# The first norm of the last layer in two halves of 128 columns, and the mean of every norm squared by ScalarE

## The reference, cut to what matters

```python
for i in range(DEPTH):                      # DEPTH = 4, D_MODEL = 1024
    last = i == DEPTH - 1
    h_lat = x_lat * (1.0 + m_lat[:, 1]) + m_lat[:, 0]
    h_ctx = x_ctx * (1.0 + m_ctx[1]) + m_ctx[0]
    y_lat, y_ctx = mixer(i, h_lat, h_ctx)   # attention or gated linear attention, then @ w_o
    x_lat = layer_norm(alpha * x_lat + m_lat[:, 2] * y_lat, ln1_g[i], ln1_b[i])
    h_lat = x_lat * (1.0 + m_lat[:, 4]) + m_lat[:, 3]
    f_lat = conv_ffn(h_lat, ffn_w_up[i], ffn_conv_w[i], ffn_conv_b[i], ffn_w_down[i])
    x_lat = layer_norm(alpha * x_lat + m_lat[:, 5] * f_lat, ln2_g[i], ln2_b[i])
    if not last:
        ...                                 # the same for the context

def layer_norm(x, g, b):                    # over the 1024 features of a token
    mu = mean(x); var = mean((x - mu) ** 2)
    return (x - mu) * rsqrt(var + LN_EPS) * g + b
```

## Time and profile before

| | us |
|---|---|
| median of three runs | 2580.01 |
| lowest and highest of them | 2573.11, 2580.82 |
| the profiled execution, its own time | 2578.89 |
| its span in the trace | 2577.1 |
| TensorE busy in it | 2438.4 (95 %) |
| VectorE busy | 1392.1 (54 %) |
| ScalarE busy | 1134.2 (44 %) |
| GpSimd busy | 334.9 (13 %) |

### The profile page before, as it was taken

One profiled execution on the slowest core, in us unless ns is written; L12 is line 12 of the kernel. 1 busy time (PEld: TensorE's weight loads), 2 busy tenths in 40 slices (PEclk: granted clock), 3 DMA queues, 4 the chain that ended last, 5 costly groups with the idle time before them and its releaser, 6 DMA issues.

```text
span 2577.1 us, 37987 instructions
## 1 busy us (share of the span) xinstructions
PE 2438.4 (95%) x15310; PEld 1960.5 (76%) x15310; DVE 1392.1 (54%) x2099; ACT 1134.2 (44%) x1936; POOL 334.9 (13%) x270
## 2 busy tenths in 40 slices
PE   6999899999999898999999999899999999978997
PEld 3655877778789558777788878787777888947997
DVE  2375665453444776555534336766555435477874
ACT  3375543333342565333323444454333325276663
POOL 0000311110100003111101003331111111002111
PEclk8999899999999999999999999999999999999998
DMA  7712366663232002665632421025666335603663
GB/s 246 213 42 81 92 182 186 180 178 105 78 99 88 28 25 66 187 181 180 176 104 80 112 69 43 2 67 150 186 185 181 113 92 105 149 17 101 186 180 99
DMA packets 500995, 311.39 MB, mean 121 GB/s; under 512 B 24194, under 2 KB 499762, under 8 KB 500692
## 3 DMA queue, kind: packets, MB, share of 16 engines
q1 hardware_dynamic: 498048, 307.39, 41.0%
q10 hardware_dynamic: 2772, 1.56, 0.2%
HBM read 307.87 MB, written 1.05 MB: 120 GB/s over the span
## 4 chain that ended last, share of the span: by engine, by line
PE 82%; DVE 7%; ACT 5%; DMA 3%; issue 2%; SPq 1%; ACTq 0%; DVEq 0%
PE bank L1543 69%; PE bank L1595 4%; PE bank L1722 2%; PE bank L1770 1%; DMA slab_raw<-in_d_w_qkv 1%; PE bank L1742 1%; DMA slab_raw<-in_a_w_o 1%; ACT slab_hi L526 1%; DVE stat L1184 1%; DVE slab_lo L960 1%; ACT p L707 1%; ACT hb L541 1%; DVE q_part L1243 1%; DMA slab_raw<-in_mod_w 1%; ACT pt L719 1%
## 5 line engine op out<-in xcount | busy, mean ns | idle before, releaser
L1543 PE MATMUL bank<-h_hi,slab_hi 128*128 128x512 f32 (+1 forms) x2416 | 859.6, 356 | 38.7 <-DVE slab_lo L960 26.5
L1543 PE MATMUL bank<-h_lo,slab_hi 128*128 128x512 f32 (+1 forms) x2416 | 836.9, 346 | 0.0
L960 DVE TENSOR_TENSOR slab_lo<-slab_raw,slab_hi 128x1024 fp32r<-128x1024 f32 (+1 forms) x388 | 538.6, 1390 | 552.1 <-ACT slab_hi L526 550.7
L1543 PE MATMUL bank<-h_hi,slab_lo 128*128 128x512 f32 (+1 forms) x2416 | 836.6, 346 | 0.0
L526 ACT ACTIVATE slab_hi<-slab_raw 128x1024 fp32r<-128x1024 f32 (+1 forms) x388 | 401.5, 1036 | 529.1 <-PE bank L1543 264.1
L1543 PEld LDWEIGHTS bank<-h_hi,slab_hi 128*128 128x128 f32 x2416 | 465.1, 193 | 150.0 <-issue 90.2
L1543 PEld LDWEIGHTS bank<-h_hi,slab_lo 128*128 128x128 f32 x2416 | 465.3, 193 | 55.9
L1543 PEld LDWEIGHTS bank<-h_lo,slab_hi 128*128 128x128 f32 x2416 | 465.9, 193 | 50.0 <-issue 0.5
L929 ACT ACTIVATE conv<-bank,prm 128x512 f32<-128x512 f32 (+1 forms) x176 | 127.3, 723 | 355.1 <-PE bank L1543 354.8
L1543 PE MATMUL bank<-g_hi,slab_hi 128*128 128x512 f32 (+1 forms) x770 | 269.3, 350 | 2.1 <-ACT res_t L577 2.1
L1543 PE MATMUL bank<-g_hi,slab_lo 128*128 128x512 f32 (+1 forms) x770 | 267.2, 347 | 0.0
(11 more groups left out here) (218 smaller groups left out, 2744.0 us busy)
## 6 DMA issues: line engine op xcount, KB each, us to landing
slab_raw<-in_mod_w SPq DMA_DIRECT2D x192, 512.0 KB, 4.5
slab_raw<-in_ffn_w_up SPq DMA_DIRECT2D x176, 512.0 KB, 4.6
slab_raw<-in_ffn_w_down SPq DMA_DIRECT2D x64, 512.0 KB, 4.1
slab_raw<-in_ffn_w_down SPq DMA_DIRECT2D x32, 384.0 KB, 3.5
slab_raw<-in_b_w_qkv SPq DMA_DIRECT2D x24, 512.0 KB, 3.8
slab_raw<-in_c_w_in SPq DMA_DIRECT2D x24, 512.0 KB, 3.8
slab_raw<-in_d_w_qkv SPq DMA_DIRECT2D x24, 512.0 KB, 7.0
slab_raw<-in_a_w_qkv SPq DMA_DIRECT2D x12, 512.0 KB, 5.4
```

Source lines behind the costliest of these rows:

```text
L960: nc.vector.tensor_tensor(wlo[slot][:, 0:w], raw[of][:, 0:w], whi[slot][:, 0:w].bitcast(f32), ALU.subtract).then_inc(s_lo, 1)
L1543: ins = mm(out, l, r, start=first and n == 0, stop=last and n == 2)
```

## The change

Three things are edited.

1. `halves(6)` becomes two parts, columns 256 to 383 and 384 to 511: the latents in two halves of 128. Stage 6 so takes the path with two parts: 4 tiles of the mixer's output projection for 256 columns, 4 tiles for the first 128, the same 4 for the other 128; `stats` twice, on 128 columns each; then `four_ahead` over the first four slabs of the MLP's up projection, for the first half of the columns and again for the second. `hb`, which holds 256 columns, is used as far as a part is wide. `segs` gives the columns of a part cut at 256, and its first number (which of the two modulation vectors) stays 1 for both halves. The code that took the single part of stage 6 through `modulate` and `last_part` goes.
2. In the block of TensorE, `whole` is counted anew for the stage behind the MLP, since stages 6 and 7 now differ.
3. In every norm ScalarE squares the mean straight from PSUM (`acc_s`), behind the copy of the mean, with a semaphore of its own; VectorE waits for it and subtracts `acc_s` from the mean square in PSUM. The instruction of L1015 is gone from VectorE. There are 15 norms of a part now, where there were 14.

```diff
 def halves(st):
-    return [slice(CTX, T)] if st // 2 == DEPTH - 1 else [slice(0, CTX), slice(CTX, T)]
+    if st == 2 * DEPTH - 2:
+        return [slice(CTX, CTX + P), slice(CTX + P, T)]
+    return [slice(CTX, T)] if st == 2 * DEPTH - 1 else [slice(0, CTX), slice(CTX, T)]
 def make_events(st):
     ...
-    return [Event(dt, slice(0, T), None, False) for dt in range(whole)] + [
+    return [Event(dt, slice(halves(st)[0].start, T), None, False) for dt in range(whole)] + [
...
         def segs(c):
-            return [s for s in ((0, slice(0, CTX)), (1, slice(CTX, T))) if s[1].start < c.stop and c.start < s[1].stop]
+            both = ((0, slice(0, CTX)), (1, slice(CTX, T)))
+            return [(s, slice(max(x.start, c.start), min(x.stop, c.stop))) for s, x in both if x.start < c.stop and c.start < x.stop]
...
             def normaliser(st, p):
                 c, n = halves(st)[p], parts_before(st, p) + 1
                 act.wait_ge(s_stats, n)
                 nc.scalar.activation(mean[:, c], LN_SUM[:, c], ACT.Copy).then_inc(s_mean, 1)
+                nc.scalar.activation(acc_s[:, c], LN_SUM[:, c], ACT.Square).then_inc(s_msq, 1)
                 act.wait_ge(s_var, n)
...
                 residual(st, fg)
-                if i + 1 == layers:
-                    for pr in range(PAIRS):
-                        modulate(st + 1, 0, pr)
...
             def variance(st, p):
                 c = halves(st)[p]
                 dve.wait_ge(s_stats, parts_before(st, p) + 1)
-                dve.wait_ge(s_mean, parts_before(st, p) + 1)
-                link(nc.vector.scalar_tensor_tensor(acc_s[:, c], mean[:, c], -1.0, mean[:, c], ALU.mult, ALU.mult))
-                link(nc.vector.tensor_tensor(acc_q[:, c], LN_SQ[:, c], acc_s[:, c], ALU.add))
+                dve.wait_ge(s_msq, parts_before(st, p) + 1)
+                link(nc.vector.tensor_tensor(acc_q[:, c], LN_SQ[:, c], acc_s[:, c], ALU.subtract))
                 nc.vector.tensor_scalar(acc_q[:, c], acc_q[:, c], 0.0, LN_EPS, ALU.max, ALU.add).then_inc(s_var, 1)
...
                 residual(st, start["wo", i][1])
-                if i + 1 == layers:
-                    last_part(st + 1, 0)
...
                 fg = start["down", i][1]
+                whole = sum(ev.part is None for ev in events[st + 1])
```

More of the change, by code:

```diff
@@ L310, in build_program @@
             "mean_ready", "var_ready", "rstd_ready", "centred", "xn_ready"))
+        s_msq = sem("mean_squared")
         s_cond_z, s_x1 = sem("cond_cleared"), sem("latents_modulated")
@@ L540, in modulate @@
                     for k in range(2):
-                        ins = nc.scalar.activation(hb[b][:, k, :], xn[:, 2 * pr + k, c], ACT.Identity,
+                        ins = nc.scalar.activation(hb[b][:, k, 0:c.stop - c.start], xn[:, 2 * pr + k, c], ACT.Identity,
                                                    bias=cf[:, 2 + s, 2 * pr + k:2 * pr + k + 1],
@@ L547, in modulate @@
                     act.wait_ge(s_x1, pr + 1)
-                nc.scalar.activation(h_hi[:, 2 * pr:2 * pr + 2, c], hb[b][:], ACT.Copy).then_inc(s_hhi, 1)
+                nc.scalar.activation(h_hi[:, 2 * pr:2 * pr + 2, c], hb[b][:, :, 0:c.stop - c.start], ACT.Copy).then_inc(s_hhi, 1)
             def normaliser(st, p):
@@ L1002, in rest @@
                 dve.wait_ge(s_hhi, n + 1)
-                nc.vector.tensor_tensor(h_lo[:, 2 * pr:2 * pr + 2, c], hb[n % 2][:],
+                nc.vector.tensor_tensor(h_lo[:, 2 * pr:2 * pr + 2, c], hb[n % 2][:, :, 0:c.stop - c.start],
                                         h_hi[:, 2 * pr:2 * pr + 2, c].bitcast(f32), ALU.subtract).then_inc(s_hlo, 1)
```

## The result

Slower, by more than forecast. The changed kernel takes **2599.66 us** (median of 7 runs, 2593.41 to 2602.76), beside 2580.82 us for the kernel before in as many (2573.11 to 2585.31): ratio **1.0071**, 95 % interval 1.0057 to 1.0086. Forecast were 2586.0 us and a range that ended at 2597; slower by over 0.3 % had a chance of 0.45, and no change 0.50. The profiled execution took 2600.32 us, 21.4 more than the 2578.89 of before; its span is 2598.5 us.

What follows compares the result with a forecast made beforehand. TensorE was taken as the bound, busy 95 % of the span. The halves' +13.9 us and the square's -6.9 us made +7.0 us on 2578.9, given as 2586 us, range 2572 to 2597.

Steps and rivals of the forecast that it cites:

- Part 1, the pace: Stage 6 and first four up slabs: 384 float32r matmuls of 128 columns, bounded by weight loads, 0.112 us each, 43.0 us.
- Rival A: Same stretch: a narrow float32r matmul is cheaper than a load alone, 0.06 to 0.09 us; kernel 2573 to 2579; chance 0.13.
- Rival B: Same stretch: narrow float32r matmuls fall to plain float32's 0.22 us each, needing a second pass; kernel about 2623; chance 0.16.
- Part 2, the waits: Stage 6 in halves: TensorE still waits 3.5 us (bounds 1 and 7.2); the second half's norm lies under matmuls.
- Part 2, the clock: Stage 6 in halves: a lower granted clock costs 1.0 us (0 to 2.5), sized by stage 2's stretch.
- Parts 1 and 2: Stretch from stage 6's output projection through the first four up slabs: 60.9 us against 47.0, +13.9 us.
- the two terms for a low clock: Stage 6's stretch: 1.0 us lost to a low clock after the change, 1.4 us lost before it.
- Part 3, the square: All norms: squaring the mean on ScalarE lets VectorE go on earlier; -6.9 us (-2 to -11).
- Rival C: All norms: the square gives nothing, as VectorE meets the next centring each time; kernel 2592; chance counted within the forecast's 0.68.
- The sum: Whole kernel: +13.9 us for the halves and -6.9 us for the square make +7.0 us, forecast 2586 us.

Runs made afterwards that it cites:

- e4: Kernel before, with layer 3's first four up slabs projected in halves of 128 columns (192 narrow matmuls for 96 wide ones): 2608.13 us, ratio 1.0118.
- e10: e4 with 17 idle matmuls ahead of the narrow ones and one ahead of each of the next two `h_lo` waits: 2586.47 us, ratio 1.0032.
- e11: Kernel before, with layer 3's first two up slabs left wide and the next four projected in halves of 128 columns: 2588.44 us, ratio 1.0039.
- e5: Changed kernel with one, two and two idle matmuls meant for the three waits inside stage 6's norm: 2578.95 us, ratio 1.0001.
- e6: e1 with 14 idle matmuls ahead of layer 3's first up pair, for stage 6's wait: 2564.58 us, ratio 0.9952.
- e1: Kernel before with only the square of the mean moved to ScalarE in every norm, layer 3's first norm whole: 2566.70 us, ratio 0.9955.
- e7: e6 with idle matmuls also for the other norms, the first projection, three attentions and behind the last norm: 2572.29 us, ratio 0.9983.
- e8: e4 with 15 idle matmuls ahead of the narrow ones: 2605.8 to 2608.8 us three times, 2587.2 us once, ratio 1.0094.

## Why the prediction failed, by its steps

**Part 1, the pace, held.** Forecast 0.112 us; measured 109 records in 12.00 us, with starts 0.11 us apart (2347.08, 2347.19). Rival A (0.06 to 0.09) is out. Rival B's price of 0.22 did show up, 0.213 for 168 matmuls, but not for its reason: these are single records at a clock of 0.50, and at 1.00 the same instruction takes 0.112. The Trainium skill ("TensorE: Matmul & The Clock Gate", back-to-back issue gap) has 81 ns for a row of loads and matmuls of 128 columns, without a figure for float32r; this row, at 112 ns, does not agree.

**Part 2, the waits, held.** Forecast 3.5 us, measured 0.23 + 0.98 + 1.04 = 2.3 us, two for `h_lo` and one for `xn` (the one for `slab_lo` did not come), and the second norm is hidden as forecast.

**Part 2, the clock, is the step that failed.** It read "1.0 us for a lower clock (0 to 2.5)". Measured are 17.0 us in the stretch and 2.2 behind it. I sized it by stage 2, where 256-column matmuls bring the clock back, and moved that to a stage whose matmuls have 128 columns. The wait's length was taken as the driver (1.0 us of clock for 3.5 of waits, and in rival A 1.5 for 6 and 2 for 9.5), and what follows the wait decides. None of the rows read had a low clock with a long row of narrow float32r matmuls behind it; so the bound of 2.5 us came from the wrong kind of row, and the upper bound should have been the narrow row behind the waits at the lower clock: 192 x 0.101 = 19 us. e4, e10 and e11 show the cause: the same 192 narrow matmuls behind an open wait, behind filled waits, and behind 48 wide ones, 2608, 2586 and 2588 us. With the clock held (e5) the halves cost what Parts 1 and 2 say: e5 less e6, both with the clock up in stage 6, is 14.4 us by the medians (12.6 by the ratios). Forecast were +13.9, and +14.3 without the two terms for a low clock (1.0 after, 1.4 before).

**Part 3, the square, was too small.** Forecast -6.9 (-2 to -11), measured -11.6 us (e1; its interval, 7.7 to 15.5, just leaves out 6.9). The waits answer to the forecast: behind stage 1 4.43 became 3.52 (forecast 3.6), in stage 2 2.45 became 1.39 (-1.06 against -1.3), at the end 9.82 became 9.11 (forecast 9.2). These rows are of the changed kernel; e1 has 3.48, 1.39 and 9.11 at the same places.

```profile
705.51 0.36 PE L1542 MATMUL bank<-h_hi,slab_hi 128*128 128x256 f32 x1 [3.52 <-DVE slab_lo L962]
989.51 0.36 PE L1542 MATMUL bank<-h_hi,slab_hi 128*128 128x256 f32 x1 [1.39 <-DVE slab_lo L962]
2589.67 1.11 PE L2063 MATMUL bank<-cst,out_f 128*128 128x128 f32 x4 [9.11 <-ACT out_f L945]
```

Three times each and once makes 6.6 us. In stage 6 of e1, where TensorE waits as before, it gained 0.6 us more, which was not in the forecast as stage 6 is in halves there. ScalarE, VectorE and GpSimd of e1 in that norm, to be read against the earlier trace rows; the last row is the `h_lo` of the kernel before:

```profile
2347.62 0.38 ACT L553 ACTIVATE mean<-bank 128x256 f32<-128x256 f32 x1 [1.54 <-PE bank L1620]
2347.90 0.38 ACT L554 ACTIVATE acc_s<-bank 128x256 f32<-128x256 f32 x1
2348.38 0.42 DVE L1017 TENSOR_TENSOR acc_q<-bank,acc_s 128x256 f32<-128x256 f32 x1 [2.41 <-ACT acc_s L554]
2348.84 0.65 DVE L1018 TENSOR_SCALAR acc_q<-acc_q 128x256 f32<-128x256 f32 x1
2348.08 5.90 POOL L1485 TENSOR_TENSOR xn<-xn,mean 128x512 f32<-128x512 f32 x4 [4.39 <-ACT mean L553]
2353.00 1.52 DVE L1005 TENSOR_TENSOR h_lo<-hb,h_hi 128x512 fp32r<-128x512 f32 x1
...
2363.98 0.69 DVE L1003 TENSOR_TENSOR h_lo<-hb,h_hi 128x512 fp32r<-128x512 f32 x1
```

The last step of the variance starts 1.22 us behind the mean, where it was 2.50 (2359.69 - 2357.19): 1.3 us earlier, as forecast. Of that `h_lo` gives back 0.8, for it now meets GpSimd's last centring and takes 1.52 us instead of 0.69. It ends 6.9 us behind the mean instead of 7.5.

The other 4.4 us of the 11.6 are the clock again, as far as two traces can show it: behind shorter waits it was low for less time. TensorE's 8 us behind stages 1, 3 and 5, first in the kernel before and then in e1:

```profile
709.09:717.09 8.00, 8.00 (x48) 7.79 (x49) 6.35 (x9) 6.37 (x12) 1.20 (x1) 0.79 0.46 133
1409.86:1417.86 8.00, 8.00 (x39) 7.73 (x40) 5.78 (x9) 6.40 (x12) 0.12 (x1) 0.64 0.49 131
2139.96:2147.96 8.00, 8.00 (x38) 7.68 (x39) 5.69 (x8) 6.39 (x12) 0.00 (x0) 0.62 0.23 68
...
706.95:714.95 8.00, 7.75 (x56) 7.25 (x57) 6.76 (x10) 6.03 (x12) 2.10 (x2) 1.00 0.46 135
1403.54:1411.54 8.00, 8.00 (x48) 7.73 (x49) 6.41 (x10) 6.14 (x12) 1.14 (x1) 0.79 0.49 132
2133.75:2141.75 8.00, 7.75 (x56) 7.25 (x57) 6.76 (x10) 6.03 (x12) 2.10 (x2) 1.00 0.24 68
```

e1 starts 8, 9 and 18 matmuls more, 35 in all, and at 0.120 us each that is 4.2 us. This is one execution against one, and in other stages the clock went both ways (0.5 for 3.4 us in stage 2 of e1, where it was low before and not in the changed kernel), so the size is less sure than the cause. Rival C (the square gives nothing) is out; by its own terms, 2586 + 6.9, it should have read 2593.

**The sum.** +13.9 and -6.9 should have been about +32 and -12. From the terms: 13.9 - 1.0 + 17.0 + 2.2 - 1.2 (shorter waits) = 30.9. The misses are of opposite sign, so the sum was off by less than its terms, and both are the same omission: the granted clock was priced as a small correction, where it is a cost of its own with its own cause.

## What to carry to other kernels

A wait on TensorE costs its own length and what the clock does behind it. Ask what runs next: 256-column float32r matmuls had brought the clock back after 2 to 6 us of their own (some 10 of them in e4, 28 in e1), and 128-column ones had not after 40. So don't put a row of narrow matmuls behind a wait; put wide ones first, or fill the wait with matmuls that nobody reads. Put these ahead of the instruction that waits: behind it they may still hold the clock (two of e5's five), but they cost their own time (e7). And splitting a float32r row into halves of 128 costs 0.104 us for each wide matmul here (2 x 0.112 - 0.120) even at the full clock, so it pays only if the wait it hides is longer.

## What the runs showed of the chip

- At a granted clock of 0.50, float32r matmuls of 128 and of 256 columns take the same 0.213 us; at 1.00 they take 0.112 and 0.120. So at the lower clock a narrow matmul does half the columns of a wide one in the same time.
- A row of narrow float32r matmuls kept the clock that it found: 1.00 for 20 us (e11) and 17 us (e10), 0.50 for 32 us (the changed kernel) and 40 us (e4), with TensorE busy without a gap in all four. The Trainium skill ("TensorE: Matmul & The Clock Gate", Part 1) says that the clock is released by how busy the engine has been. By the busy time in the records that would have brought the narrow rows back like the wide ones, and the runs speak against it; what the chip counts in its place stays open.
- Whether the clock falls at small waits varies from execution to execution: one and the same kernel (e8) took 2587 us at a mean granted clock of 0.983, and 2606 to 2609 us at 0.971 to 0.973.
- It varies within an execution too: behind waits of 3.48 us each, at stages 1 and 3 of e1, the granted clock over the next 8 us was 1.00 and 0.79.
